# Sums over partitions of one head: one float32 product replaced by two products of rounded halves

## The reference, cut to what matters

```python
def l2_normalize(x, eps=NORM_EPS):
    return x * lax.rsqrt(jnp.sum(x * x, axis=-1, keepdims=True) + eps)
# q, k: convolution, silu, then l2_normalize; attention q: rms_norm per head
gc = jnp.cumsum(g.reshape(B, H, N, C), axis=-1)
diff = gc[..., :, None] - gc[..., None, :]
decay = jnp.where(tril, jnp.exp(jnp.where(tril, diff, 0.0)), 0.0)
...
o = (o_fwd + o_bwd).transpose(0, 2, 1, 3)
o = rms_norm(o) * norm_w * gate
```

## Time and profile before

| | |
|---|---|
| median of 3 runs | 2704.25 us (2702.0 to 2705.16) |
| the profiled execution | 2706.94 us, span 2705.2 us |
| PE busy | 2603.7 us, 96% of the span |
| DVE busy | 1408.0 us, 52% |
| ACT busy | 1029.2 us, 38% |
| POOL busy | 214.4 us, 8% |
| loads of `ada_w`, issue to landing | 4.4 us |

### The profile page before, as it was taken

One profiled execution on the slowest core, in us unless ns is written; L12 is line 12 of the kernel. 1 busy time (PEld: TensorE's weight loads), 2 busy tenths in 40 slices (PEclk: granted clock), 3 DMA queues, 4 the chain that ended last, 5 costly groups with the idle time before them and its releaser, 6 DMA issues.

```text
span 2705.2 us, 35982 instructions
## 1 busy us (share of the span) xinstructions
PE 2603.7 (96%) x12454; PEld 2130.1 (79%) x12454; DVE 1408.0 (52%) x1830; ACT 1029.2 (38%) x1438; POOL 214.4 (8%) x286
## 2 busy tenths in 40 slices
PE   4899999999999989989999999999999999999997
PEld 4777887888888868866888888887888888888885
DVE  3644666666666666455444444444344443444454
ACT  5224354354354344334443234442244432232334
POOL 2320211211211212000000000000000000000000
PEclk9888999999999989999999999999999999999998
DMA  8752544544544535432332333333333333333333
GB/s 289 273 171 61 156 124 125 155 122 127 155 119 129 152 87 155 128 85 73 98 101 82 95 102 93 101 92 91 103 94 93 98 88 93 103 98 93 88 91 125
DMA packets 431810, 318.47 MB, mean 118 GB/s; under 512 B 12902, under 2 KB 403857, under 8 KB 431249
## 3 DMA queue, kind: packets, MB, share of 16 engines
q1 hardware_dynamic: 401648, 212.19, 27.3%
q0 software_dynamic: 29184, 104.87, 12.2%
q10 hardware_dynamic: 929, 0.74, 0.1%
HBM read 313.56 MB, written 4.19 MB: 117 GB/s over the span
## 4 chain that ended last, share of the span: by engine, by line
PE 92%; DVE 3%; DMA 2%; ACT 1%; issue 1%; DVEq 0%; ACTq 0%; POOL 0%; POOLq 0%
PE pw L1355 23%; PE pw L1357 22%; PE pw L1356 22%; PE pw L1339 2%; PE pw L1341 2%; PE pw L1340 2%; PE pd L1622 2%; PE pd L1645 1%; PE pd L1658 1%; PE pd L1605 1%; DMA EG<-in_w_ada_dram 1%; PE pd L1665 1%; PE pd L1419 1%; DMA va<-in_w_ada_dram 1%; PE pd L1449 1%
## 5 line engine op out<-in xcount | busy, mean ns | idle before, releaser
L1355 PE MATMUL pw<-act_hi,w_hi 128*128 128x512 f32 x2016 | 814.9, 404 | 14.9 <-DVE act_lo L1250 8.8
L907 DVE TENSOR_TENSOR w_lo<-raw,w_hi 128x1024 fp32r<-128x1024 f32 x426 | 520.8, 1223 | 544.2 <-ACT w_hi L547 541.7
L1357 PE MATMUL pw<-act_hi,w_lo 128*128 128x512 f32 x2016 | 789.1, 391 | 0.0
L1356 PE MATMUL pw<-act_lo,w_hi 128*128 128x512 f32 x2016 | 787.3, 391 | 0.0
L547 ACT ACTIVATE w_hi<-raw 128x1024 fp32r<-128x1024 f32 x426 | 450.2, 1057 | 543.2 <-PE pw L1357 427.0
L1355 PEld LDWEIGHTS pw<-act_hi,w_hi 128*128 128x128 f32 x2016 | 380.5, 189 | 108.2 <-issue 24.7
L1357 PEld LDWEIGHTS pw<-act_hi,w_lo 128*128 128x128 f32 x2016 | 380.0, 188 | 82.2
L1356 PEld LDWEIGHTS pw<-act_lo,w_hi 128*128 128x128 f32 x2016 | 380.8, 189 | 80.1 <-issue 6.9
L1355 PE MATMUL pw<-mh_hi,w_hi 128*128 128x512 f32 x704 | 280.4, 398 | 1.1 <-DVE w_lo L907 1.1
L1356 PE MATMUL pw<-mh_lo,w_hi 128*128 128x512 f32 x704 | 278.3, 395 | 0.0
L1357 PE MATMUL pw<-mh_hi,w_lo 128*128 128x512 f32 x704 | 278.3, 395 | 0.0
(11 more groups left out here) (280 smaller groups left out, 2684.3 us busy)
## 6 DMA issues: line engine op xcount, KB each, us to landing
raw<-in_w_up_dram SPq DMA_DIRECT2D x176, 512.0 KB, 3.9
ada_w<-in_w_ada_dram POOLq DMA_DIRECT2D x128, 512.0 KB, 4.4
raw<-in_w_in_dram SPq DMA_DIRECT2D x84, 512.0 KB, 3.9
raw<-in_w_down_dram SPq DMA_DIRECT2D x64, 384.0 KB, 3.4
raw<-in_w_down_dram SPq DMA_DIRECT2D x64, 320.0 KB, 3.1
raw<-in_w_out_dram SPq DMA_DIRECT2D x32, 512.0 KB, 4.4
DD<-in_w_ada_dram POOLq DMA_DIRECT2D x8, 512.0 KB, 8.4
mixed<-in_x_dram SPq DMA_DIRECT2D x4, 1024.0 KB, 13.8
```

The source lines that it names most:

```text
L907: V.tensor_tensor(w_lo[slot][:], raw[slot][:], w_hi[slot][:].bitcast(F32), ALU.subtract).then_inc(lo_made.sem, 1)
L1355: M(bank, w_hi[slot][:, k, :], hi[:, k0 + k, :], start=first, stop=False)
L1356: M(bank, w_hi[slot][:, k, :], lo[:, k0 + k, :], start=False, stop=False)
L1357: ins = M(bank, w_lo[slot][:, k, :], hi[:, k0 + k, :], start=False, stop=last)
```

## The change

A second way to make the six sums. The float32 values are cut into a high half rounded to float32r and the rest, also float32r, and each sum is two float32r products with a float32r copy of the ones (`ones_r`), accumulated in the same bank.
- Decay: DVE makes the halves of the log decay for all heads once before head 0 (`g_halves`). POOL multiplies the masks with both halves (`decay_terms`, four 128x512 multiplies) for head h+1 at the end of its list for head h, and for head 0 before its first head. DVE's two multiplies go. The tiles `CLr`, `Tr` lie in the memory of `CL` and `T`, so POOL waits for `z_sum` and `vn_sum` of head h.
- Squares: ACT computes each of the four squares twice, once in float32 and once with a float32r output (`sq_high`, `o_high`), and DVE subtracts (`square_low`, `o_low`). PE waits for the lower halves.
- PE makes `ada_sums` of the head before ahead of `run(0, 8)`, where it stood behind it; DVE's `ada_columns` moves from behind `s(1)` to behind the second convolution.

```diff
-        gu_made = signal("gu_made", 2)
+        gu_made = signal("gu_made", 4)
...
+            def decay_terms(h, after):
+
+                upto = cst[:, C_CUM:C_CUM + 2 * P].rearrange("p (d n) -> p d n", n=P)
+                for i, to in enumerate((CLr, Tr)):
+                    if after is not None:
+                        pool.wait_ge(*(z_sum, vn_sum)[i].after(after))
+                    for d in range(2):
+                        g = g_halves[:, i, :, d, bass.ds(h, 1)].bitcast(F32)
+                        nc.gpsimd.tensor_tensor(to[:, d].rearrange("p (b n) -> p b n", n=P),
+                                                upto[:, d].unsqueeze(1).broadcast_to([P, NB, P]),
+                                                g.broadcast_to([P, NB, P]), ALU.mult).then_inc(gu_made.sem, 1)
...
+                if not last:
+                    decay_terms(h + 1, h)
...
+            act.wait_ge(consts_in, 16)
             act.wait_ge(*c_sum.after(0))
+            nc.scalar.activation(ones_r[:], ones, ACT.Copy)
             nc.scalar.activation(cond[:], pd[3][:, 0:KT], ACT.Silu).then_inc(cond_made.sem, 1)
...
                 nc.scalar.activation(sqa, at(mixedf, h), ACT.Square).then_inc(sq_done.sem, 1)
+                nc.scalar.activation(sq_high[2], at(mixedf, h), ACT.Square).then_inc(sq_high_made.sem, 1)
...
                         nc.scalar.activation(tmp[:, part, :], act3[:, part, :], ACT.Square).then_inc(sq_done.sem, 1)
+                        nc.scalar.activation(sq_high[part], act3[:, part, :], ACT.Square).then_inc(sq_high_made.sem, 1)
...
                 nc.scalar.activation(tmp[:, 0, :], pd[4], ACT.Square).then_inc(onorm.sem, 1)
+                nc.scalar.activation(o_high, pd[4], ACT.Square).then_inc(o_high_made.sem, 1)
...
-            dve.wait_ge(*gate_v.after(0))
+            dve.wait_ge(*gate_v.after(0, 8))
+
+            V.tensor_copy(g_halves[:, 0], gall[:, 1]).then_inc(gate_v.sem, 1)
+            dve.wait_ge(*gate_v.after(0, 9))
+            V.tensor_tensor(g_halves[:, 1], gall[:, 1], g_halves[:, 0].bitcast(F32), ALU.subtract).then_inc(gate_v.sem, 1)
...
-                for d in range(2):
-                    V.tensor_tensor(CL[:, d], cst[:, C_CUM + d * P:C_CUM + (d + 1) * P].unsqueeze(1).broadcast_to([P, NB, P]),
-                                    gcur[:, 1, :, d].unsqueeze(2).broadcast_to([P, NB, P]), ALU.mult).then_inc(gu_made.sem, 1)
+
+                def square_low(i):
+
+                    full = (tmp[:, 0, :], tmp[:, 1, :], sqa)[i]
+                    dve.wait_ge(*sq_high_made.after(h, (2, 3, 1)[i]))
+                    V.tensor_tensor(sq_low[i], full, sq_high[i].bitcast(F32), ALU.subtract).then_inc(sq_low_made.sem, 1)
...
+                    if part == 1:
+                        if not first:
+                            ada_columns(h - 1)
+                        square_low(2)
+                        square_low(0)
+                square_low(1)
                 if out:
                     low_halves(0)
 
                 s(1)
-                if not first:
-                    ada_columns(h - 1)
...
+                dve.wait_ge(*o_high_made.after(h))
+                V.tensor_tensor(o_low, tmp[:, 0, :], o_high.bitcast(F32), ALU.subtract).then_inc(o_low_made.sem, 1)
                 dve.wait_ge(*onorm.after(h))
...
-                run(0, 8)
                 if not first:
                     ada_sums(h - 1)
+                run(0, 8)
                 pe.wait_ge(*gu_made.after(h))
                 for d in range(2):
-                    M(pd[d], ones, one(CL[:, d]), start=True, stop=True).then_inc(gc_sum.sem, 1)
+                    M(pd[d], ones_r[:], CLr[:, d], start=True, stop=False)
+                    M(pd[d], ones_r[:], Tr[:, d], start=False, stop=True).then_inc(gc_sum.sem, 1)
                 run(8, 14)
 
-                pe.wait_ge(*sq_done.after(h, 2))
-                M(pd[3], ones, tmp[:, 0, :], start=True, stop=True).then_inc(ss_sum.sem, 1)
+                pe.wait_ge(*sq_low_made.after(h, 2))
+                M(pd[3], ones_r[:], sq_high[0], start=True, stop=False)
+                M(pd[3], ones_r[:], sq_low[0], start=False, stop=True).then_inc(ss_sum.sem, 1)
...
-                pe.wait_ge(*onorm.after(h, 1))
-                M(pd[2], ones, tmp[:, 0, :], start=True, stop=True).then_inc(sso_sum.sem, 1)
+                pe.wait_ge(*o_low_made.after(h))
+                M(pd[2], ones_r[:], o_high, start=True, stop=False)
+                M(pd[2], ones_r[:], o_low, start=False, stop=True).then_inc(sso_sum.sem, 1)
```

More of the change, by code:

```diff
@@ L51 @@
 LEVELS = 7
+UNDER_SPLITS = 2 * KV_HEADS * S + 2 * HEADS * S + 3 * ADA_W + LEVELS * P // 2 + 3 * (S + 2) + 3 * S + 2 * S + 2 * S + 4 * S
 C_N = C_PAR + 2 * LEVELS
@@ L171, in build @@
         gcur = sb("gcur", [P, 4, NB, 2], F32, mixer)
+        g_halves = sb("g_halves", [P, 2, NB, 2, HEADS], F32R, mixer)
+        ones_r = sb("ones_r", [P, P], F32R, mixer)
         glast = sb("glast", [P, 2, NB], F32, mixer)
@@ L175, in build @@
         mixer.close()
+        split_in = ExitStack()
+        sb("under_splits", [P, UNDER_SPLITS], F32, split_in)
+        CLr = sb("CLr", [P, 2, S], F32R, split_in)
+        Tr = sb("Tr", [P, 2, S], F32R, split_in)
+        PTr = sb("PTr", [P, 4, S], F32R, split_in)
+        XTr = sb("XTr", [P, S], F32R, split_in)
+        sb("under_qr", [P, S], F32, split_in)
+        qrr = sb("qrr", [P, S], F32R, split_in)
+        split_in.close()
         two = lambda t: t.rearrange("p d b n -> p (d b n)")
@@ L231, in build @@
         pd23 = pdt[:, 2:4, :].rearrange("p a n -> p (a n)")
+        sq_high = [PTr[:, i] for i in (0, 1, 2)]
+        sq_low = [XTr[:], qrr[:], PTr[:, 3]]
+        o_high, o_low = sq_high[0], sq_high[1]
         blocks = lambda t: t.rearrange("p (b n) -> p b n", n=P)
@@ L304, in build @@
         gcur_made = signal("gcur_made")
-        gu_made = signal("gu_made", 2)
+        gu_made = signal("gu_made", 4)
+        sq_high_made, sq_low_made = signal("sq_high_made", 3), signal("sq_low_made", 3)
+        o_high_made, o_low_made = signal("o_high_made"), signal("o_low_made")
         gap_masked = signal("gap_masked")
@@ L373, in build @@
         ba_sum, cum_sum = signal("ba_sum"), signal("cum_sum")
-        gate_a, gate_v = signal("gate_a", 5), signal("gate_v", 8)
+        gate_a, gate_v = signal("gate_a", 5), signal("gate_v", 10)
         kv_sq, kv_ss, kv_rstd = signal("kv_sq", 1), signal("kv_ss", 1), signal("kv_rstd", 2)
@@ L497, in ada_load, with head @@
                     .then_inc(ada_in[k % 2], 16)
-            def head(h, first=False):
+            def decay_terms(h, after):
[8 more added lines that the diff above has]
+                                                g.broadcast_to([P, NB, P]), ALU.mult).then_inc(gu_made.sem, 1)
+            def head(h, first=False, last=False):
                 loads = {0: (2,), 1: (3,), 2: (4,), 3: (5, 6), 4: (7, 8), 5: (9, 10), 6: (11, 12, 13, 14, 15)}
@@ L513, in head @@
                         ada_load(h, k)
+                if not last:
+                    decay_terms(h + 1, h)
+            pool.wait_ge(more_in, 16)
+            pool.wait_ge(*gate_v.after(0))
+            decay_terms(0, None)
             head(0, first=True)
-            with pool.Fori(1, HEADS) as h:
+            with pool.Fori(1, HEADS - 1) as h:
                 head(h)
+            head(HEADS - 1, last=True)
             pool.wait_ge(*av_sum.after(HEADS - 1))
```

10 lines of the change are left out of this document (6 added, 4 removed).

## The result

| | before | after |
|---|---|---|
| median (15 runs each, on one chip) | 2705.16 us (2702.0 to 2709.7) | 2709.44 us (2706.3 to 2713.0) |
| ratio | | 1.0015, interval 1.0008 to 1.0022 |
| the profiled execution, span | 2706.94, 2705.2 | 2708.2, 2706.5 |

What follows compares the result with a forecast made beforehand. PE, busy 96% of the span, was taken as the bound. Head 0 -1.65, heads 1 to 6 -7.4, head 7 +2.6 and its sum of o -0.4 gave -6.85: from 2704.25 to 2697.4 us, range 2689.5 to 2704.5.

Steps and rivals of the forecast that it cites:

- A sum costs 0.40 less on PE; 2.5 a head.: PE's sums: two float32r products replace one float32 product, saving 0.40 us a sum, 2.5 a head if PE never waits.
- EG starts 14.9 to 15.1 us behind the sum of o.: Heads 1 to 6: `EG`, behind the third silu and a table load, keeps about its old distance of 15.17 us.
- PE waits 0.35 us for q's lower half.: Heads 1 to 6: PE waits 0.35 us for DVE's third subtraction before its second square sum.
- The waits of 0.52 and 0.21 us on DVE go, and the factors are ready at 577.2.: DVE's chain to `T`, heads 1 to 6: its waits for PE vanish, so inverse factors come at 577.2, not 577.99.
- The rule holds and POOL alone pays; no cost.: POOL's multiplies beside DVE: the engines contend when DVE reads two SBUF inputs, but only POOL slows, costing nothing.
- A head keeps 1.2 us: Heads 1 to 6: after PE's wait for `T`, 1.2 us of the 2.5 saved remains, six times: 7.4 us.
- Head 7 loses 2.6.: Head 7: `act_lo` starts 3.8 us later, the three square sums give 1.2 back, so +2.6 us.
- Head 0 gains 2.1 from PE's start.: Head 0: five cheaper sums count in full, -2.1 us; `g_halves` ahead of PE's start adds 0.45.
- Behind 1.88 us of idle the durations stayed short.: PE's clock at row 1080.15: no slowdown followed this idle time; the slowdown decides from a wait of about 2 us.
- the third rival: Heads 1 to 6: PE idles over 2 us at once, its clock falls, some 1.8 us more each; 2715.6, 5 in 100.
- The front swallows it: Heads 1 to 6: squares or subtraction delay the third convolution 1.2 us more, gaining 0; 2704.8 us, 18 in 100.
- the three signs that I named for being wrong: No PE wait in the loop's heads; head 7's `act_lo` less than 2 us later; sum records not stepping by 0.23.

Runs made afterwards that it cites:

- z2: Changed kernel with head 7's order, later ada step, moved decay multiplies, more projection products before the first square sum, square subtractions behind the third convolution: 2691.72 us, ratio 0.9947.
- x1: Changed kernel without POOL's mask multiplies of levels 0 and 1, ACT writing zeros instead (output not the reference's): 2701.27 us, ratio 0.9983.
- z1: Changed kernel with DVE's second ada step of each head ahead of the first score maximum instead of behind it: 2704.39 us, ratio 0.9995.
- x2: Changed kernel with POOL's decay multiplies for heads 1 to 7 moved behind ada_w loads 12 and 13, plus a DVE wait for `gc_sum`: 2708.95 us, ratio 1.0010.
- x4: Changed kernel with DVE's second ada step of each head moved from ahead of `T` to behind the first score normalization: 2703.19 us, ratio 0.9985.
- x3: Changed kernel with DVE, in head 7 alone, making `act_lo` right behind the third convolution, ahead of the squares' lower halves: 2704.45 us, ratio 0.9996.

## Why the prediction was wrong, step by step

- *A sum costs 0.40 less on PE; 2.5 a head.* The size of a sum was right: the records step by 542.15 - 541.91 = 0.24. In z2, where PE waits for nothing listed up to there, the first product with normalized tiles starts 18.56 us behind the sum of o, and 20.94 before: 2.4 of the 2.5. But not all of it could be kept. At `T` z2 is ahead by only 1.9; of the 0.5 that came back on the way, 0.3 is the wait for the rotated q. PE's busy time fell by 17.3 us in all, not 20; it holds modelled ends, so it isn't a measure of the same thing.
- *EG starts 14.9 to 15.1 us behind the sum of o.* 15.21 measured; some 0.14 of the 1.05 us by which `T` missed its forecast.
- *PE waits 0.35 us for q's lower half.* 0.52, 0.48 in the mean. Right in kind.
- *The waits of 0.52 and 0.21 us on DVE go, and the factors are ready at 577.2.* **This is the step that failed.** The waits did go. But DVE's rotation multiply, no longer held up by PE, now starts while POOL's level 0 multiply runs, and the ada step, 0.53 us ahead of POOL's level 1 multiply before, starts 0.42 us behind it. They took 0.6 and 0.5 more, and `T` was ready 31.96 us behind the sum of o (572.47 + 1.40 - 541.91), where it was 31.70 before and 30.9 forecast. x1 gives 1.13 us of a period back by removing POOL alone, z1 gives 0.56 by the order of two instructions. In the prediction's terms the overlap was wrong: DVE's instructions were counted at their old lengths at moments when POOL is now at work.
- *The rule holds and POOL alone pays; no cost.* Wrong, in the reading, not in the row: POOL paid in the kernel before because it came second. The note that DVE might pay 0.6 us for the subtraction of o was right for that instruction (1.28), and the sum of o did not wait for it. But DVE's copy of vn ahead of it did come late, by 0.2 us a head (x2).
- *A head keeps 1.2 us* came from the last two, and is the term that was lost, 8.9 us: -7.4 forecast, +1.5 measured. The period was forecast at 100.4 and x1 and x4, without the collision or without the step that suffers most from it, show 100.8. The 0.4 us that is left isn't taken apart; waits in it that the forecast had smaller or not at all are q's lower half (0.48 for 0.35), the copies of vn (0.2) and, in x4, the rotated q (0.26).
- *Head 7 loses 2.6.* Right, by its mechanism: `act_lo` started 3.6 us later (3.8 forecast), as DVE waited for ACT's high square of k. The wait was 17.6 us, not some 14: PE has 3.1 us less to do ahead of it, since the decay sums no longer run at the low clock (3.78 us before), and that time only went into the wait. The cost was avoidable: x3 takes it away with the order of four calls.
- *Head 0 gains 2.1 from PE's start.* 1.8. There POOL's four multiplies ran beside DVE's first convolution (1.35 us for 0.48, 2.88 for 1.54), hidden by `run(0, 8)`. That no collision ahead of `T` came on top was luck, by 0.17 us (see x2): in the profile of x3 the same head gained only 0.9.
- *Behind 1.88 us of idle the durations stayed short.* True of the kernel before; in the changed one 1.6 us went to the clock at that place, behind 1.90 us. So the dividing line at a wait of about 2 us, which the third rival took, does not hold.
- *The rivals.* "The front swallows it" gave 2704.8 and the right symptom, `T` as late as before, by the wrong mechanism: the third convolution was not late. I had named contention and given it no price ahead of `T`, where both engines work side by side in every head; that rival was missing. None of the three signs that I named for being wrong came about, so they could not have shown this failure; the period of 101.95 for 100.4 does.

## What to carry to other kernels

When a wait on one engine goes, redraw which instructions of the others lie beside it: two that shared a port in a harmless order may swap, and the one on the critical path then stands for the rest of the other's instruction. Price DVE's instructions with two SBUF inputs beside POOL's by who starts first, and keep POOL's multiplies away from the chain that PE waits for, or put an instruction without need for the chain (the ada step) behind it. Work that takes a piece from PE and gives a piece to a front engine (the squares) is only as good as that engine's slack; the part that unloads both (the decay) shortened the period by itself. And an order that holds by a tenth or two of a microsecond isn't safe: the same code can meet the other case in the next execution.

## What the runs showed of the hardware that was not expected

- POOL and DVE exclude each other for whole instructions, where DVE reads two tiles. Times alone and when second, DVE: 0.68 to 1.29, 1.28 to 1.82, 1.88 and 2.22, 1.22 to 1.72; POOL: 1.16 to 1.78, 1.92 and 2.14. DVE's scaling of one tile by a column, 0.48 alone, took 1.35 beside POOL in head 0, so two tensor inputs are not needed for it (its record starts 0.02 us ahead of POOL's, too close to tell which was first).
- POOL's multiply of two float32 tiles with broadcasts into float32r takes 1.03 us, less than the 1.16 of its multiply by a bf16 mask.
- The same wait of 1.88 to 1.90 us was followed by some eight products at half the clock in nine profiles and by none in five; each of the two kernels that were profiled twice did the same both times. What decides it is open.
